# Delta rule: the triangular inverses of two token tiles in one 128x128 matrix

## The reference, cut to what matters

```python
k_beta = k * beta[..., None]
a = jnp.einsum("bhncd,bhnsd->bhncs", k_beta, k) * decay        # 64 x 64 for each head and chunk
t_mat = jnp.eye(C) + jnp.where(strict, a, 0.0)                 # unit lower triangular
rhs = jnp.concatenate([v_beta, k_beta * jnp.exp(g)[..., None]], axis=-1)
sol = lax.linalg.triangular_solve(t_mat, rhs, left_side=True, lower=True, unit_diagonal=True)
u, w = sol[..., :Dv], sol[..., Dv:]
```

## Time and profile before

| | us |
|---|---|
| median of three runs | 2551.4 |
| lowest and highest | 2549.64, 2551.79 |
| profiled execution, its time | 2551.56 |
| span of that execution | 2549.7 |
| PE busy in the span | 2535.2 (99%) |
| DVE busy | 1515.0 (59%) |
| ACT busy | 1070.4 (42%) |
| stage of the inverses (1242.02 to 1330.03) | 88.01 |

### The profile page before, as it was taken

How to read it: one execution, slowest core, us unless ns; L and a number is a source line. 1 busy time by engine, 2 the same in 40 slices (tenths; PEclk the granted TensorE clock), 3 DMA queues, 4 the chain that set the end, 5 groups by cost and what they waited for, 6 DMA issues and landing times.

```text
span 2549.7 us, 27853 instructions
## 1 busy us (share of the span) xinstructions
PE 2535.2 (99%) x11712; PEld 2105.0 (83%) x11712; DVE 1515.0 (59%) x1273; ACT 1070.4 (42%) x878; POOL 107.7 (4%) x170
## 2 busy tenths in 40 slices
PE   9999999999999999999999999999999999999998
PEld 7888888888888888888888888887888888888887
DVE  5465655544455545688678997644555544455544
ACT  5454443433333334555325445543444333334333
POOL 0000000000000000122000101200000000000000
PEclk9999999999999999999999999999999999999999
DMA  8644666755566757777334466853666666566764
GB/s 303 219 168 142 218 219 212 221 194 198 193 222 213 228 189 226 248 235 210 116 100 149 149 188 211 245 165 115 209 217 218 203 212 196 198 209 221 230 193 137
DMA packets 158892, 506.15 MB, mean 199 GB/s; under 512 B 15824, under 2 KB 43088, under 8 KB 157616
## 3 DMA queue, kind: packets, MB, share of 16 engines
q1 hardware_dynamic: 152912, 484.96, 59.5%
q0 software_dynamic: 5440, 18.89, 2.3%
q10 hardware_dynamic: 416, 0.52, 0.1%
HBM read 465.51 MB, written 4.19 MB: 184 GB/s over the span
## 4 chain that ended last, share of the span: by engine, by line
PE 97%; DVE 1%; ACT 1%; DMA 0%; issue 0%; SPq 0%; POOLq 0%; POOL 0%; ACTq 0%
PE ps L820 30%; PE ps L821 30%; PE ps L824 30%; PE ps L1053 1%; PE ps L1264 1%; PE ps L1280 1%; DVE weights_lo L1788 1%; PE ps L790 0%; PE ps L959 0%; DVE conv_out L2069 0%; PE ps L1125 0%; PE ps L1190 0%; PE ps L1030 0%; PE ps L1021 0%; PE ps L853 0%; PE ps L1199 0%
## 5 line engine op out<-in xcount | busy, mean ns | idle before, releaser
L1788 DVE TENSOR_TENSOR weights_lo<-weights_raw,weights_hi 128x2048 fp32r<-128x2048 f32 x431 | 986.5, 2290 | 886.9 <-ACT weights_hi L1344 886.9
L1344 ACT ACTIVATE weights_hi<-weights_raw 128x2048 fp32r<-128x2048 f32 x431 | 825.2, 1916 | 1222.9 <-PE ps L824 1162.9
L820 PE MATMUL ps<-weights_hi,stationary_hi 128*128 128x512 f32 x2408 | 945.1, 393 | 2.5 <-ACT stationary_hi L1361 1.1
L821 PE MATMUL ps<-weights_lo,stationary_hi 128*128 128x512 f32 x2408 | 937.3, 389 | 0.0
L824 PE MATMUL ps<-weights_hi,stationary_lo 128*128 128x512 f32 x2408 | 741.7, 389 | 0.0
L820 PEld LDWEIGHTS ps<-weights_hi,stationary_hi 128*128 128x128 f32 x2408 | 452.2, 188 | 97.9 <-issue 3.5
L824 PEld LDWEIGHTS ps<-weights_hi,stationary_lo 128*128 128x128 f32 x2408 | 452.0, 188 | 94.6
L821 PEld LDWEIGHTS ps<-weights_lo,stationary_hi 128*128 128x128 f32 x2408 | 452.3, 188 | 92.8 <-issue 0.7
L820 PE MATMUL ps<-weights_hi,hidden_hi 128*128 128x512 f32 x1008 | 392.1, 389 | 0.0
L821 PE MATMUL ps<-weights_lo,hidden_hi 128*128 128x512 f32 x1008 | 392.1, 389 | 0.0
L824 PE MATMUL ps<-weights_hi,hidden_lo 128*128 128x512 f32 x1008 | 310.3, 389 | 0.0
(11 more groups left out here) (342 smaller groups left out, 1065.8 us busy)
## 6 DMA issues: line engine op xcount, KB each, us to landing
weights_raw<-in_w SPq DMA_DIRECT2D x128, 1024.0 KB, 5.5
weights_raw<-in_w_in SPq DMA_DIRECT2D x79, 1024.0 KB, 5.4
weights_raw<-in_w_up SPq DMA_DIRECT2D x64, 1024.0 KB, 5.0
weights_raw<-in_w_down SPq DMA_DIRECT2D x64, 1024.0 KB, 5.5
weights_raw<-in_w_out SPq DMA_DIRECT2D x32, 1024.0 KB, 5.5
hidden<-turned_blocks SPq DMA_DIRECT2D x328, 64.0 KB, 2.8
weights_raw<-in_wk SPq DMA_DIRECT2D x16, 1024.0 KB, 5.5
weights_raw<-in_wv SPq DMA_DIRECT2D x16, 1024.0 KB, 5.5
```

Of the source, the lines that this page charges most:

```text
L820: pe.matmul(o, xh, WHI[:, slot, j, c * BANK:(c + 1) * BANK], start=first and j == 0, stop=False)
L821: pe.matmul(o, xh, WLO[:, low, j, c * BANK:(c + 1) * BANK], start=False, stop=False)
L1344: act.activation(WHI[:, s % NSPLIT], RAW[:, s % NRAW], ACT.Copy).then_inc(hi_ready, 1)
L1788: dve.tensor_tensor(WLO[:, s % NRAW], RAW[:, s % NRAW], WHI[:, s % NSPLIT].bitcast(F32), ALU.subtract).then_inc(lo_ready, 1)
```

## The change

The second token tile's matrix of a head is put, not transposed, in the other triangle of the first tile's matrix. So a pair matrix has tile 0's chunks (as LT gives them) in the triangles on one side and tile 1's transposed problem on the other, in the same 64x64 diagonal blocks. Eight pairs replace sixteen units. Tile 1's eight LT matrices are transposed by PE in the middle of ga's last step and added to tile 0's. Masks are new: in each level the odd and even blocks belong to different triangles, so `halves_of` keeps one triangle of each block of X and of X^T (XM and XN), and `OFF_DIAGONAL` keeps the neighbouring blocks of the product. Each level's product LT·XM, its masking and XN·WL are eight matmuls and operations of 1024 columns in place of 2048. The levels start one step later (steps 2 to 6 in place of 1 to 5); the first (2x2) level needs no transposes by PE now. In the last level both XN·WL and WL·XN are made, and the 32x32 corners of each go into tile 0's and tile 1's half of `inverse_t`, negated, by ACT and DVE; the rest of `inverse_t` is X^T and X masked with TRI. v_tok times beta moves to gb's step 7. Four of the masks come by a DMA of their own between the loads of ga and gb, as `squares` has 15 matrices now.

```diff
+    mats = [ident, tri, same, negmask, np.ones((P, P)), (i[:, None] ^ 1) == i[None, :]]
+    levels = [2 ** n for n in range(1, LEVELS)]
+    for b in levels:
+        r, c = block(b)
+        mats.append((r == c) & np.where(r % 2 == 0, i[:, None] >= i[None, :], i[:, None] <= i[None, :]))
+    for b in levels[:-1]:
+        r, c = block(b)
+        mats.append((r ^ 1) == c)
...
# SP
-                        sp.dma_start(SQ[:, 1:, :], squares[:, 1:, :]).then_inc(sq_landed, 16)
+                        sp.dma_start(SQ[:, 1:, :], squares[:, 1:11, :]).then_inc(sq_landed, 16)
...
+            sp.wait_ge(ba_out, 1)
+            sp.dma_start(OFF_DIAGONAL[:], squares[:, 11:, :]).then_inc(sq_landed, 16)
             load_pass(S_IN2 + 5 * PS, w_in2, IN2_COLS[5])
...
# PE
+            def pairs(lhs, rhs, bank):
+                for h in range(PAIRS):
+                    last = pe.matmul(ps[:, bank + h // 4, (h % 4) * P:(h % 4 + 1) * P], lhs[:, h, :], rhs[:, h, :], start=True, stop=True)
                 return last
...
             def during_ga(k, j):
+                if (k, j) == (7, 1):
+                    pe.wait_ge(gram_ready, 2)
+                    for h in range(HEADS):
+                        last = pe.transpose(ps[:, 4 + h // 4, (h % 4) * P:(h % 4 + 1) * P], LT[:, HEADS + h, :], IDENT)
+                    last.then_inc(lp_turned, 1)
...
             def during_gb(k, j):
-                if (k, j) == (0, 1):
...
-                elif 1 <= k < LEVELS:
+                if 2 <= k <= LEVELS:
                     if j == 0:
-                        pe.wait_ge(x_up, k)
-                        units(LT, XI).then_inc(wl_done, 1)
+                        pe.wait_ge(xm_ready, k - 1)
+                        pairs(LT, XM, 4).then_inc(w_done, 1)
+                    elif k < LEVELS:
+                        pe.wait_ge(wl_ready, k - 1)
+                        pe.wait_ge(xn_ready, k - 1)
+                        pairs(XN, WL, 6).then_inc(xw_done, 1)
                     else:
+                        pe.wait_ge(inv_a, 1)
+                        pe.wait_ge(xn_ready, k - 1)
+                        pairs(WL, XN, 4)
+                        pairs(XN, WL, 6).then_inc(inv_done, 1)
...
-            pe.wait_ge(xt_up, LEVELS)
+            pe.wait_ge(inv_a, 2)
+            pe.wait_ge(inv_b, 2)
...
# ACT, gb, behind the split of step 6
+                elif k == LEVELS:
+                    act.wait_ge(w_done, k - 1)
+                    act.wait_ge(xw_done, k - 2)
+                    act.activation(WL[:], ps[:, 4:6, :].rearrange("p b (u c) -> p (b u) c", c=P), ACT.Copy).then_inc(inv_a, 1)
+                    act.wait_ge(inv_done, 1)
+                    act.wait_ge(inv_b, 1)
+                    for r in (0, CHUNK):
+                        rows, cols = slice(r, r + SIDE), slice(r + SIDE, r + CHUNK)
+                        last = act.activation(XT[rows, 0:PAIRS, cols], ps[rows, 4:6, :].rearrange("p b (u c) -> p (b u) c", c=P)[:, :, cols],
+                                              ACT.Copy, scale=-1.0)
+                    last.then_inc(inv_a, 1)
...
# DVE, ga, step 7
-                        dve.tensor_tensor(heads(VTOK), heads(VTOK), per_head(beta[:]), ALU.mult).then_inc(v_ready, 1)
+                        dve.wait_ge(lp_turned, 1)
+                        dve.wait_ge(gram_ready, 1)
+                        own.mark(dve.tensor_tensor(LT[:, 0:PAIRS, :], LT[:, 0:PAIRS, :], w_units, ALU.add))
+                        own.wait()
+                        own.mark(dve.tensor_tensor(WL[:], LT[:, 0:PAIRS, :], each_pair(SQ[:, 5, :]), ALU.mult))
...
# DVE, gb
             for k in range(PS):
+                xpt = XT[:, 0:PAIRS, :]
+                if k == 0:
+                    left(S_IN2 + 5 * PS, P_IN2 + 4, GA[:, 1, :], N_IN2)
+                    own.wait()
+                    own.mark(dve.tensor_tensor(xpt, eye, WL[:], ALU.subtract))
+                elif k == 1:
+                    own.wait()
+                    dve.tensor_tensor(XM[:], XP[:], halves_of(1), ALU.mult).then_inc(xm_ready, 1)
+                elif k <= LEVELS:
+                    if k > 2:
+                        own.mark(dve.transpose(flat(xpt), flat(XP[:])))
+                        own.wait()
+                        dve.tensor_tensor(XN[:], xpt, halves_of(k - 1), ALU.mult).then_inc(xn_ready, 1)
+                    if k < LEVELS:
+                        dve.wait_ge(w_done, k - 1)
+                        dve.wait_ge(sq_landed, 32)
+                        dve.tensor_tensor(WL[:], w_units, each_pair(OFF_DIAGONAL[:, k - 2, :]), ALU.mult).then_inc(wl_ready, 1)
+                    else:
+                        dve.wait_ge(xn_ready, k - 1)
+                        dve.tensor_tensor(xpt, xpt, each_pair(TRI), ALU.mult).then_inc(inv_b, 1)
+                        own.mark(dve.tensor_tensor(XT[:, PAIRS:, :], XP[:], each_pair(TRI), ALU.mult))
                 split_next(S_IN2 + 5 * PS + k)
                 if k == 0:
+                    own.wait()
+                    own.mark(dve.transpose(flat(XP[:]), flat(xpt)))
+                elif k == 1:
+                    dve.tensor_tensor(XN[:], xpt, halves_of(1), ALU.mult).then_inc(xn_ready, 1)
+                elif k < LEVELS:
+                    dve.wait_ge(xw_done, k - 1)
+                    own.mark(dve.tensor_tensor(XP[:], XP[:], xw_units, ALU.subtract))
+                    own.wait()
+                    dve.tensor_tensor(XM[:], XP[:], halves_of(k), ALU.mult).then_inc(xm_ready, 1)
+                elif k == LEVELS:
+                    dve.wait_ge(inv_done, 1)
+                    own.wait()
+                    for r in (0, CHUNK):
+                        rows, cols = slice(r, r + SIDE), slice(r + SIDE, r + CHUNK)
+                        last = dve.tensor_scalar(XT[rows, PAIRS:, cols], xw_units[rows, :, cols], -1.0, None, ALU.mult)
+                    last.then_inc(inv_b, 1)
+                else:
+                    dve.tensor_tensor(heads(VTOK), heads(VTOK), per_head(beta[:]), ALU.mult).then_inc(v_ready, 1)
```

More of the change, by code:

```diff
@@ L44 @@
 LOG_TERMS = 8
+LEVELS = 6
 NEG = -1e30
@@ L54, in shape_constants @@
     negmask = np.where(tri, 0.0, NEG)
[L55 to L60, removed]
+    mats = [ident, tri, same, negmask, np.ones((P, P)), (i[:, None] ^ 1) == i[None, :]]
+    block = lambda b: (i[:, None] // b, i[None, :] // b)
+    levels = [2 ** n for n in range(1, LEVELS)]
[5 more added lines that the diff above has]
+        mats.append((r ^ 1) == c)
     squares = np.stack([np.asarray(m, np.float32) for m in mats], 1)
@@ L125, in build @@
         IDENT, TRI, SAME, NEGMASK, ONES = (SQ[:, n, :] for n in range(5))
-        LEVELS = 6
         NORMS = 10
@@ L207, in build @@
         ATT = units_at("attn_t", 4)
-        XI = units_at("inverse", 0)
         XT = units_at("inverse_t", 3)
-        WL = units_at("level_product", 7)
+        PAIRS = HEADS
+        XP = at("inverse", [P, PAIRS, P], slot(0))
+        XM = at("inverse_half", [P, PAIRS, P], slot(0) + 4)
+        WL = at("level_product", [P, PAIRS, P], slot(7))
+        XN = at("inverse_half_t", [P, PAIRS, P], slot(7) + 4)
+        OFF_DIAGONAL = at("level_masks", [P, LEVELS - 2, P], slot(10) + 4)
         KBG = at("k_beta_decayed", [P, TT, HEADS, HD], slot(0))
@@ L366, in build @@
         gram_ready = sem("gram_ready")
-        level0_ready = sem("level0_ready")
-        level0_turned = sem("level0_turned")
-        wl_done = sem("wl_done")
+        lp_turned = sem("lp_turned")
+        xm_ready = sem("xm_ready")
+        xn_ready = sem("xn_ready")
+        w_done = sem("w_done")
         wl_ready = sem("wl_ready")
         xw_done = sem("xw_done")
-        x_up = sem("x_up")
-        xt_done = sem("xt_done")
-        xt_up = sem("xt_up")
+        inv_done = sem("inv_done")
+        inv_a = sem("inv_a")
+        inv_b = sem("inv_b")
         glu_ready = sem("glu_ready")
@@ L1049, in turn_back @@
                 last.then_inc(done, 1)
-            def units(lhs, rhs):
-                for u in range(U16):
-                    last = pe.matmul(ps[:, 4 + u // 4, (u % 4) * P:(u % 4 + 1) * P], lhs[:, u, :], rhs[:, u, :], start=True, stop=True)
+            def pairs(lhs, rhs, bank):
+                for h in range(PAIRS):
+                    last = pe.matmul(ps[:, bank + h // 4, (h % 4) * P:(h % 4 + 1) * P], lhs[:, h, :], rhs[:, h, :], start=True, stop=True)
                 return last
@@ L1129, in during_gb @@
             def during_gb(k, j):
-                if (k, j) == (0, 1):
[L1132 to L1136, removed]
-                elif 1 <= k < LEVELS:
-                    if j == 0:
-                        pe.wait_ge(x_up, k)
-                        units(LT, XI).then_inc(wl_done, 1)
-                    else:
-                        pe.wait_ge(wl_ready, k)
-                        pe.wait_ge(xt_up, k)
-                        if k < LEVELS - 1:
-                            units(XT, WL).then_inc(xw_done, 1)
-                        else:
```

(19 more changed lines are left out.)

29 lines of the change are left out of this document (9 added, 20 removed).

## The result

The changed kernel takes 2531.25 us (median of four, 2531.06 to 2531.65) against 2550.97 for the one before (2549.64 to 2551.79): a ratio of 0.9923, 95% interval 0.9911 to 0.9935, 19.7 us or 0.8% less. The forecast was 2531.3.

The account below looks back on a forecast made before the run. PE, busy 99% of the span, was taken as the bound. Savings of 2.43 + 2.25 + 0.05 + 15.7 = 20.4 us less 0.3 of waits gave 20.1, so 2531.3 us; range 2529.0 to 2536.0.

Parts of the forecast that it names:

- The count of matmuls: PE's inverse blocks: eleven of eight matmuls take 19.2 us against 34.9 for ten of sixteen, saving 15.7.
- Rival D: Inverse blocks on PE: eight matmuls cost more than half of sixteen; 0.2 us more per block gives 2533.5; chance 0.05.
- The transposes: Sixteen low-clock PE transposes (3.30 us) become eight at full clock in ga's last step (0.87), saving 2.43, without a wait.
- The gap: PE's 2.25 us loss before the sixteen transposes goes, as gb's first step no longer waits for an inverse.
- What hides the rest: DVE's start-up work before gb's step 1 is covered by 0.4 us; end-of-pass work costs at most 0.3.
- The bound of the waits: PE's four waits for the masked half (k = 3 to 6), 0.3 us in all: at most 1.0 if operations take 1.31.
- Rival A: PE's clock falls at the new waits, 1.55 us each: 2537.5 at all four levels, 2532.9 at one; chance 0.05.
- B: DVE's start-up chain is late and PE waits: worst case 2533.9 us, with one clock fall; chance 0.08.
- C: DVE sets the level if half-width operations cost as much as full width: 25 us lost, 20.4 saved, 2556; chance 0.02.

Follow-up runs that it names:

- the heaps: Two groups of times of the unchanged kernel before, over all series: 26 up to 2550.9 us and 30 from 2551.1 us on.

## Why the prediction was right

- **The count of matmuls.** Forecast 19.2 for eleven blocks and 0.3 of waits; measured five of 1.70, four of 1.81 and 3.48, 19.22 with the waits in it. The term was 0.4 high in the blocks and 0.1 low in the waits (0.11 four times, just over "0.05 to 0.1"). The blocks give 15.7 of the 20.5 us, and the run with doubled matmuls, where the gain is gone, shows that it is their count. Rival D (a price of its own for a block) has the wrong sign: a short block is 0.09 cheaper.
- **The transposes.** 0.79 for 0.87, no wait for the Gram product, clock 1.00. The 0.87 was half of the chain's row of 1.75, which doesn't count from start to start. PE's timeline of the kernel before has for the same sixteen transposes:

```profile
1203.36 1.91 PE L959 MATMUL ps<-squares,k_tok 128*128 128x128 f32 x16
1205.02 0.48 PE L820 MATMUL ps<-weights_hi,stationary_hi 128*128 128x512 f32 x1
```

From start to start that is 1.66. With it the low clock costs 3.30 - 1.66 = 1.64 and not 1.55, and it could have been seen ahead that sixteen rows alone cost less than half of 3.49 (1.70 for 1.745 in the blocks): this is what was wrong in the block term and in the argument against rival D.

- **The gap.** It went, and with it the wait; without it and otherwise unchanged, the kernel before is 3.6 faster. Here the prediction took too much from one profile: "this one wait cost 2.25 + 1.55 us" holds for the execution that it read. In another the same gap left the clock alone. So the clock's 1.6 is paid in about half of the executions, as the heaps suggest (30 of 56), and by an estimate from that 0.9 on the average. The forecast was a difference from the profiled execution's own time, which had the low clock, so its absolute time came out right. Against an execution without it the same sum has to leave the 1.55 out. That it came out within 0.1 us is luck in part: the stage was 0.4 shorter than forecast (67.47 for 67.9), and 0.2 was lost ahead of it.
- **What hides the rest.** The split for step 1 ended at 1250.68, PE came at 1251.30 (forecast: 0.4 of cover, and it is 0.48 with 0.14 for the signal). With v_tok behind the mask it was used up, and PE paid in the two places worked out, with 0.1 less in all. The end of the pass came as counted back: the last split ends 1.45 behind the pass (1308.87 + 2.29 - 1309.71), and moves nothing.
- **The bound of the waits** took 1.31 for the slowest 1024-wide operations of DVE; no row has it. The slowest kind takes 1.28, and in the stage the transposing form takes 1.24. So the 1.0 was too wide.
- **Rival A** (clock) did not come: the waits of 0.11 left the clock at 1.00, as did four gaps of 1.10. **B** has its mechanism shown, but not in the change. **C** fell with the durations: 1.22 for each half-width operation, and DVE idle 0.9 to 1.1 us before each subtraction. It comes near when PE's part shrinks: in quadrants DVE has no idle time left between the levels, and its cover is used up at the last.

The sum of the stage: gap 2.25, transposes 3.30 - 0.79 = 2.51, blocks 34.9 - 19.2 = 15.7, together 20.5, and 20.54 is measured. The 15.7 has the waits of 0.44 in it.

## What to carry to other kernels

On an engine that is busy 99% of the time, count its instructions by differences of start times and look for who waits only afterwards; one short wait there is worth reading at the clock too, in more than one execution. Don't take a length from one view and a difference of starts from another. Before narrowing a small f32 matmul ask what its row costs: here half as many matmuls paid, half the moving columns did not. Two independent 64x64 blocks ran cheapest as two products on quadrants of their own; whether the smaller load or the overlap did it was not told apart.

## What the runs showed of the hardware

- A gap of 2.1 us on PE was followed by the lower clock level (0.50 during the sixteen transposes) in one profile and not in another of the same kernel; the one gap of 0.95 and the four of 1.10, each in one profile, were not.
- Thirty-two rows of f32 matmuls with 128x128 weights take 3.48 us, 109 ns each, with 64 and with 128 moving columns. Sixteen alone take 1.70, and sixteen more in the same block 1.79.
- Rows of 64x64 weights on the two diagonal quadrants take 34 ns each in the mean (1.08 us for thirty-two).
- A wait of 0.11 us is in no list of the matmuls' waits; it shows as a block that is 0.11 longer, and in the weight loads' list, with 0.26 us of idle time before the block's first load.
